# Attention values as a stationary block of high and low parts, in a two-layer kernel on one core

## The chip, the cores and the metric

One core of one Trainium2 chip runs the kernel. The metric is device time in microseconds (us) from one launch; lower is better. The times of before are the median of three runs.

## The reference

One block of a mixer, a gated feed-forward network and a per-layer embedding gate runs over 256 positions of width 2048 in fp32, then one layer of sliding-window attention with sinks. Only the attention layer's mixer is touched here:

```python
# D_MODEL 2048, 32 heads of 64, 4 key/value heads (8 query heads each), blocks of 128 positions
q, k, v, gate = split(h @ w_in, [2048, 2304, 2560])
q, k = rms_norm(q, q_gain), rms_norm(k, k_gain)       # per head of 64
s = einsum('bqhgd,bkhd->bhgqk', qj, kb) * scale + bias  # query block j, keys of blocks j-1 and j
s = where(valid, s, -inf)
m = maximum(max(s), sink)
p = exp(s - m)
p = p / (sum(p) + exp(sink - m))
o = einsum('bhgqk,bkhd->bqhgd', p, vb)
return (o * silu(gate)) @ w_out
```

So each query block weighs one or two blocks of 128 values, each head's row is divided by its denominator, and the result is multiplied by the silu of a gate and projected.

## The kernel before

Each engine has its own instruction stream, run strictly in order; semaphores tie them together.

**Large products.** All weights come in chunks of 256 rows by 512 columns (512 KB) through a ring of 8 buffers `w_raw`. To keep fp32 precision with faster products, each operand x is split into a high part (`w_hi`, rounded to the type F32R by ScalarE, L473) and a low part (`w_lo`, x minus high, by VectorE, L771). TensorE then issues three products 128x512 per piece: high times low, high times high, low times high (`chunk`, L1239 on; 12 products per chunk: 2 blocks of positions, 2 row blocks, 3 products). Split buffers are a ring of four (SPL), so ScalarE's split of chunk s waits until TensorE has used chunk s-4. Eight chunks are a *unit*, 512 output columns; it accumulates in two banks `acc`.

**The attention layer** has 9 units (SWA_UNIT + v, v = 0 to 8: keys and values, four of queries, four of gates), followed by 4 units of the output projection (SO_UNIT). The attention of a *group* g (8 query heads that share one key/value head) is spread by hand over units v = g+3 and g+4: in each engine's loop over v and chunk c, conditions such as `if c == 3 and 3 <= v <= 6` place a step behind the split or the product of chunk c. A group has three *rounds* r: round 0 is query block 0 with 8 heads and one key block; rounds 1 and 2 are query block 1, four heads each, two key blocks. For each round:
- `score` (TensorE, L1480) writes scores into the banks `sp`; `softmax_max` (VectorE, L1126 to L1134) scales them, adds the bias, takes the maximum; `exp` (ScalarE, L695, L697) follows, with the sums.
- `turn` (TensorE, L1279): eight 128x128 transposes of the probabilities into two halves of `tp`; ScalarE's `copy` (L518) takes them to `tile[7]`.
- `weigh` (TensorE, L1499): per head and key block one plain fp32 product, 128x128 probabilities stationary, 128x64 values moving, into one half of `tp`, with positions on partitions.
- `weighted` (VectorE, L1141 to L1148): denominator, reciprocal, and the multiply of that half by it into `wide`.

When the gate's unit is done, ScalarE takes it with Silu (L480), `gated` (L1156) multiplies it in, TensorE turns the result (`to_features`, L1269), and `high` (L488) and `low` (L779) split it into `yh` and `yl` for the output projection. The queries of each group are turned the same way and copied by ScalarE.

**The two halves of tp.** All transposes and weighed outputs pass through two banks, `tp[0]` and `tp[1]`, in the order of the list HALVES. Half h may be written once half h-2 has been taken (`free(h)`, `before(h)`), told by counters `tp_left["a"]` (ScalarE) and `tp_left["d"]` (VectorE); a letter in HALVES says who takes it ("x": ScalarE reads high, VectorE then takes low). In one unit the order is: turn(g,0) 2 halves, weigh(g,0) 1, turn(g,1) 2, queries of g+1 2, weigh(g,1) 1, turn(g,2) 2, weigh(g,2) 1.

**Order on TensorE in unit v = g+3**, behind chunk c: c=0 score(g,1); c=1 weigh(g-1,2); c=2 turn(g,0), score(g,2); c=3 weigh(g,0); c=4 turn(g,1); c=5 queries of g+1; c=6 score(g+1,0), weigh(g,1); c=7 turn(g,2).

**On ScalarE**, behind split c: c=0 query copy; c=2 copy of turn(g-1,2), exp(g,0); c=3 take of the last unit; c=4 exp(g,1); c=5 copy of turn(g,0); c=6 exp(g,2); c=7 copy of turn(g,1).

**On VectorE**, behind split c: c=1 weighted(g-1,1), softmax_max(g,0); c=3 softmax_max(g,1), weighted(g-1,2); c=5 softmax_max(g,2); c=6 weighted(g,0); c=7 the queries' mean squares.

Of the kernel before, what the change touches and what calls it, by code (L numbers as in the profile page):

```python
# [20 lines left out]
F32 = mybir.dt.float32  # L21
# [5 lines left out]
P = 128  # L27
# [57 lines left out]
for _g in range(5):  # L85
    if _g == 0:
        H_Q[0] = len(HALVES)
        HALVES += "aa"
        continue
    q = _g - 1  # L90
    H_PT[q, 0] = len(HALVES); HALVES += "aa"
    H_PV[q, 0] = len(HALVES); HALVES += "d"
    H_PT[q, 1] = len(HALVES); HALVES += "aa"
    if _g < 4:
        H_Q[_g] = len(HALVES); HALVES += "aa"
    else:
        H_OG[0] = len(HALVES); HALVES += "xx"
    H_PV[q, 1] = len(HALVES); HALVES += "d"
    H_PT[q, 2] = len(HALVES); HALVES += "aa"
    H_PV[q, 2] = len(HALVES); HALVES += "d"  # L100
for _g in range(1, 4):
    H_OG[_g] = len(HALVES); HALVES += "xx"
# [47 lines left out]
def build(nc, x, p, norm_mix_g, w_in, sgu_ln_g, sgu_ln_b, sgu_w, sgu_b, sc_conv_w, cf_conv_w,  # L150
# [11 lines left out]
    with ExitStack() as ctx:  # L162
# [100 lines left out]
        og_ready = sem("og_ready")  # L263
        last_bank = sem("last_bank")
# [202 lines left out]
        def _(act):  # L467
# [230 lines left out]

            for v in range(9):
                for c in range(8):  # L700
# [16 lines left out]
                    if (v, c) == (1, 3):  # L717
                        act.wait_ge(prod, 2)
                        take(SWA_UNIT, tok(0), ACT.Copy, rr)
                    if (v, c) == (2, 6):  # L720
# [3 lines left out]
                    if c == 0 and v >= 7:  # L724
                        high(H_OG[v - 7], yh[:, 4 * (v - 7):4 * (v - 7) + 4])

                    if c == 2 and 4 <= v <= 7:
                        copy(H_PT[v - 4, 2], tile[7])
# [4 lines left out]
                    if c == 3 and v >= 6:  # L733
                        if v > 6:
                            act.wait_ge(og_ready, v - 6)
                        take(SWA_UNIT + v - 1, tok(1), ACT.Silu, rr)
                    if c == 4 and 3 <= v <= 6:
                        exp(v - 3, 1)
                    if c == 5 and 3 <= v <= 6:
                        copy(H_PT[v - 3, 0], tile[7])  # L740
                    if c == 6 and 3 <= v <= 6:
                        exp(v - 3, 2)
                    if c == 7 and 3 <= v <= 6:
                        copy(H_PT[v - 3, 1], tile[7])

            for j in range(NG):
                for c in range(8):
                    split(START[SO_UNIT + j] + c)
                    if (j, c) == (0, 0):
                        high(H_OG[2], yh[:, 8:12])  # L750
                    if (j, c) == (0, 3):
                        act.wait_ge(og_ready, 3)
                        take(SO_UNIT - 1, tok(1), ACT.Silu, rr)
                    if (j, c) == (0, 5):
                        high(H_OG[3], yh[:, 12:16])
# [3 lines left out]
        def _(dve):  # L759
# [375 lines left out]

            def weighted(g, r):

                n = 3 * g + r
                t, h0, nh, nk = ROUNDS[r]
                dve.wait_ge(expd, n + 1)  # L1140
                step(dve.tensor_tensor(rden[:, n, 0:nh], ssum[:, n, 0:nh], ssink[:, n, 0:nh], ALU.add))  # L1141
                step(dve.reciprocal(rden[:, n, 0:nh], rden[:, n, 0:nh]))
                h = H_PV[g, r]
                wait_half(dve, h)
                dst = wide[:, t, CW * g + HD * h0:CW * g + HD * (h0 + nh)].rearrange("p (h n) -> p h n", n=HD)
                src = tp[h % 2][:, 0:HD * nh].rearrange("p (h n) -> p h n", n=HD)
                by = rden[:, n, 0:nh].unsqueeze(2).to_broadcast([P, nh, HD])
                dve.tensor_tensor(dst, src, by, ALU.mult).then_inc(tp_left["d"], 1)  # L1148

            def gated(g):  # L1150

                wait_left(dve, SWA_UNIT + 5 + g)
                cols = wide[:, :, CW * g:CW * (g + 1)]
                if g == 3:
                    wait_half_left(dve, H_PV[3, 2])
                dve.tensor_tensor(cols, cols, tok(1), ALU.mult).then_inc(og_ready, 1)  # L1156

            for v in range(9):
                for c in range(8):
# [22 lines left out]
                    if (v, c) == (2, 0):  # L1182

                        wait_left(dve, SWA_UNIT)
                        kv = tok(0)[:, :, 0:256]
# [14 lines left out]
                    if c == 0 and v >= 7:  # L1200
                        q = slice(4 * (v - 7), 4 * (v - 7) + 4)
                        low(H_OG[v - 7], yl[:, q], yh[:, q])
# [12 lines left out]
                    if c == 5 and 3 <= v <= 6:  # L1215
                        softmax_max(v - 3, 2)
                    if c == 6 and 3 <= v <= 6:
                        weighted(v - 3, 0)

            for j in range(NG):  # L1220
                for c in range(8):
                    split(START[SO_UNIT + j] + c)
                    if (j, c) == (0, 0):
                        low(H_OG[2], yl[:, 8:12], yh[:, 8:12])
                    if (j, c) == (0, 3):
                        gated(3)
                    if (j, c) == (0, 5):
                        low(H_OG[3], yl[:, 12:16], yh[:, 12:16])
# [9 lines left out]
        def _(pe):  # L1238
# [252 lines left out]
            def weigh(g, r):  # L1491

                t, h0, nh, nk = ROUNDS[r]
                wait_half_left(pe, H_PT[g, r] + 1)
                h = H_PV[g, r]
                free(h)
# [4 lines left out]
                last.then_inc(tp_ready, 1)  # L1501

            for v in range(9):
                for c in range(8):
# [26 lines left out]
                    if c == 5 and v >= 6:  # L1531
                        pe.wait_ge(og_ready, v - 5)
# [51 lines left out]
```

## Time and profile before

| | us |
|---|---|
| median of 3 runs | 1452.02 (1451.65 to 1453.01) |
| the profiled execution's own time | 1451.7 |
| its span, first to last instruction | 1449.7 |
| PE busy | 1443.1 |
| VectorE (DVE) busy | 961.3 |
| ScalarE (ACT) busy | 697.3 |

The profile is of one execution. PE is TensorE's products, PEld its weight loads, DVE VectorE, ACT ScalarE, POOL GpSimd; L12 is line 12 of the kernel. Busy does not mean at full rate: the records of pipelined products overlap, so a stretch is read by the distance of starts. The chain of waits gives a product's own share of time, from its start to the next start. The trace of HBM and DMA shows 188 GB/s over the span.

### The profile page before, as it was taken

The numbers are of one execution on the slowest core, as the hardware profiler recorded it, in microseconds if no ns is written. First come the engines' busy times: TensorE is split into PE (matmuls) and PEld (weight loads), VectorE is DVE, ScalarE is ACT, GpSimd is POOL, SyncE is SP. The second block draws the span as 40 slices with busy tenths as digits, with TensorE's granted clock in tenths as the row PEclk, the third lists the DMA queues.
The fourth block names the chain that finished last, engine by engine and source line by source line (L and its number), as shares of the span: only waits on it lengthen the run. The fifth ranks groups of instructions, "written<-read, shape, count | busy, mean of one in ns | idle before, by whom it ended". The sixth has DMA issues, their size and how long they took to land.

```text
span 1449.7 us, 18187 instructions
## 1 busy us (share of the span) xinstructions
PE 1443.1 (100%) x6679; PEld 1196.2 (83%) x6679; DVE 961.3 (66%) x1318; ACT 697.3 (48%) x926; POOL 51.4 (4%) x52
## 2 busy tenths in 40 slices
PE   9999999999999999999999999999999999999999
PEld 7888888888888888888888888888888888888887
DVE  5599977956666554566754546769798567665553
ACT  7444564454444433444444344445555566564432
POOL 2000010000000000000000000000000212200000
PEclk9999999999999999999999999999999999999999
DMA  9765556666665566666655666655565755545562
GB/s 334 221 189 175 182 178 217 190 195 186 198 197 194 189 191 195 195 190 192 195 188 190 193 197 190 194 185 179 196 202 176 235 152 171 154 125 164 173 206 89
DMA packets 141494, 274.03 MB, mean 189 GB/s; under 512 B 8593, under 2 KB 10893, under 8 KB 141304
## 3 DMA queue, kind: packets, MB, share of 16 engines
q1 hardware_dynamic: 139608, 266.49, 59.2%
q0 software_dynamic: 1792, 6.71, 1.5%
q8 instruction: 39, 0.64, 0.2%
q14 instruction: 23, 0.19, 0.0%
q10 hardware_dynamic: 32, 0.01, 0.0%
HBM read 271.02 MB, written 2.15 MB: 188 GB/s over the span
## 4 chain that ended last, share of the span: by engine, by line
PE 97%; DVE 1%; ACT 1%; issue 0%; POOL 0%; POOLq 0%; ACTq 0%
PE acc L1249 31%; PE acc L1251 30%; PE acc L1250 30%; PE tp L1499 1%; PE tp L1269 1%; PE acc L1311 1%; PE sp L1480 1%; PE tp L1279 1%; DVE w_lo L771 1%; DVE tile L1126 0%; ACT tile L695 0%; ACT w_hi L473 0%; DVE smx L1130 0%; PE acc L1286 0%; PE tp L1301 0%
## 5 line engine op out<-in xcount | busy, mean ns | idle before, releaser
L771 DVE TENSOR_TENSOR w_lo<-w_raw,w_hi 128x1024 fp32r<-128x1024 f32 x500 | 610.8, 1224 | 419.9 <-ACT w_hi L473 417.3
L473 ACT ACTIVATE w_hi<-w_raw 128x1024 fp32r<-128x1024 f32 x500 | 528.5, 1060 | 609.5 <-PE acc L1251 608.2
L1249 PE MATMUL acc<-w_lo,yh 128*128 128x512 f32 x1184 | 461.6, 390 | 0.0
L1251 PE MATMUL acc<-w_hi,yl 128*128 128x512 f32 x1184 | 460.7, 389 | 0.0
L1250 PE MATMUL acc<-w_hi,yh 128*128 128x512 f32 x1184 | 460.6, 389 | 0.0
L1249 PE MATMUL acc<-w_lo,hh 128*128 128x512 f32 x784 | 309.7, 395 | 0.0
L1251 PE MATMUL acc<-w_hi,hl 128*128 128x512 f32 x784 | 305.7, 390 | 0.0
L1250 PE MATMUL acc<-w_hi,hh 128*128 128x512 f32 x784 | 305.1, 389 | 0.0
L1249 PEld LDWEIGHTS acc<-w_lo,yh 128*128 128x128 f32 x1184 | 222.3, 188 | 46.3 <-issue 0.6
L1251 PEld LDWEIGHTS acc<-w_hi,yl 128*128 128x128 f32 x1184 | 222.3, 188 | 46.3
L1250 PEld LDWEIGHTS acc<-w_hi,yh 128*128 128x128 f32 x1184 | 222.3, 188 | 46.1
L1249 PEld LDWEIGHTS acc<-w_lo,hh 128*128 128x128 f32 x784 | 147.2, 188 | 32.0 <-issue 2.3
L1251 PEld LDWEIGHTS acc<-w_hi,hl 128*128 128x128 f32 x784 | 147.2, 188 | 31.4
L1250 PEld LDWEIGHTS acc<-w_hi,hh 128*128 128x128 f32 x784 | 147.4, 188 | 29.2
L795 DVE STREAM_TRANSPOSE tile<-resid 32x256 f32<-32x256 f32 x144 | 62.7, 436 | 2.3
L795 DVE STREAM_TRANSPOSE tile<-tile 32x256 f32<-32x256 f32 x128 | 55.8, 436 | 2.1
L849 DVE SCALAR_TENSOR_TENSOR tile<-tile,cw 128x255 f32<-128x255 f32 (+29 forms) x120 | 48.1, 461 | 0.0
L431 POOL TENSOR_SCALAR eps_ms<-ms 128x2 f32<-128x2 f32 (+2 forms) x9 | 8.4, 935 | 960.1 <-DVE ms L833 917.9
L695 ACT ACTIVATE tile<-tile,negm 128x128 f32<-128x128 f32 (+1 forms) x64 | 28.3, 444 | 20.8 <-DVE ssink L1134 20.8
L518 ACT ACTIVATE tile<-tp 128x512 f32<-128x512 f32 x32 | 17.2, 589 | 30.2 <-PE tp L1279 21.9
L480 ACT ACTIVATE tile<-acc,rs 128x512 f32<-128x512 f32 x42 | 26.3, 676 | 0.0
L827 DVE TENSOR_TENSOR resid<-acc,resid 128x512 f32<-128x512 f32 x38 | 24.3, 682 | 0.3 <-PE acc L1251 0.3
(150 smaller groups left out, 559.1 us busy)
## 6 DMA issues: line engine op xcount, KB each, us to landing
w_raw<-in_w_gate SPq DMA_DIRECT2D x88, 512.0 KB, 3.7
w_raw<-in_w_up SPq DMA_DIRECT2D x88, 512.0 KB, 3.8
w_raw<-in_w_down SPq DMA_DIRECT2D x88, 512.0 KB, 4.1
w_raw<-in_swa_w_in SPq DMA_DIRECT2D x72, 512.0 KB, 3.8
w_raw<-in_w_in SPq DMA_DIRECT2D x64, 512.0 KB, 4.3
w_raw<-in_w_out SPq DMA_DIRECT2D x32, 512.0 KB, 4.2
w_raw<-in_w_ple_gate SPq DMA_DIRECT2D x32, 512.0 KB, 3.7
w_raw<-in_swa_w_out SPq DMA_DIRECT2D x32, 512.0 KB, 4.0
```

The lines of the kernel that those rows point to most:

```text
L473: act.activation(w_hi[:, s % SPL], w_raw[:, s % RAW], ACT.Copy).then_inc(hi_ready, 1)
L480: last = act.activation(dst[:, t], acc[u % 2][t][:], func, scale=s_)
L518: act.activation(dst[:, 512 * i:512 * (i + 1)], tp[(h + i) % 2][:], ACT.Copy, scale=scale).then_inc(tp_left["a"], 1)
L695: act.activation(sv[:, i], sv[:, i], ACT.Exp, bias=negm[:, n, i:i + 1], accum_out=ssum[:, n, i:i + 1])
L771: dve.tensor_tensor(w_lo[:, s % SPL], w_raw[:, s % RAW], w_hi[:, s % SPL].bitcast(F32), ALU.subtract).then_inc(lo_ready, 1)
L795: last = dve.transpose(into, block)
L827: last = dve.tensor_tensor(cols, acc[u % 2][t][:], cols, ALU.add)
L849: dve.scalar_tensor_tensor(dst, src, w_, dst, ALU.mult, ALU.add).then_inc(conv, 1)
L1249: pe.matmul(dst, xh[:, f, tk], w_lo[:, s % SPL, k], start=(f == 0), stop=False)
L1250: pe.matmul(dst, xh[:, f, tk], w_hi[:, s % SPL, k], start=False, stop=False)
L1251: last = pe.matmul(dst, xl[:, f, tk], w_hi[:, s % SPL, k], start=False, stop=(f == CK * n - 1))
L1269: last = pe.transpose(half_tile(h + i)[:, k, P * t:P * (t + 1)], src[:, t, P * f:P * (f + 1)], ident[:])
```

## The change

The values are split once into a block per key block and value head: 64 columns of high parts and 64 of low parts side by side (`v_parts`, in part of `yh` that is free then), by ScalarE behind split (1, 5) and VectorE behind (2, 0). The turned probabilities are split too: `high` by ScalarE into `pt_hi` and `low` by VectorE into `pt_lo` replace ScalarE's copy. `weigh` now holds the value block stationary and moves 512 columns of probabilities (four heads by 128 positions), high then low part; the output comes with features on partitions: 0 to 63 from the values' high parts, 64 to 127 from the low parts. ScalarE copies the lower rows out (`keep_low_rows`), VectorE adds both (`weighted`) into `out_t`, already turned. Round 0 fills two halves of `tp` instead of one. The reciprocals of the denominators are no longer multiplied into the output but into the gate (`gated`), before the gate is turned; the turned gate is multiplied into the output (`og`), and ScalarE and VectorE split that (`og_high`, `og_low`).

```diff
+        pt_hi, pt_lo = yh[:, 12:16], yl[:, 12:16]
+        v_parts = yh[:, 8:12].rearrange("p (t a) (b n) -> p t (a b) n", t=T, n=P)
+        out_t = wide[:].rearrange("p t n -> p (t n)").rearrange("p (k n) -> p k n", k=KT)
# the list of halves: who takes them
-    H_PT[q, 0] = len(HALVES); HALVES += "aa"
-    H_PV[q, 0] = len(HALVES); HALVES += "d"
-    H_PT[q, 1] = len(HALVES); HALVES += "aa"
+    H_PT[q, 0] = len(HALVES); HALVES += "xx"
+    H_PV[q, 0] = len(HALVES); HALVES += "dd"
+    H_PT[q, 1] = len(HALVES); HALVES += "xx"
...
# ScalarE
+            def keep_low_rows(g, r):
+                for i in range(2 if r == 0 else 1):
+                    wait_half(act, H_PV[g, r] + i)
+                    act.activation(tile[7][0:HD, 512 * i:512 * (i + 1)], tp[(H_PV[g, r] + i) % 2][HD:P], ACT.Copy).then_inc(
+                        pv_low, 1)
+            def og_high(g):
+                act.wait_ge(og_ready, g + 1)
+                act.activation(yh[:, 4 * g:4 * g + 4], out_t[:, 4 * g:4 * g + 4], ACT.Copy).then_inc(og_hi, 1)
...
+                    if c == 1 and 4 <= v <= 7:
+                        keep_low_rows(v - 4, 1)
                     if c == 2 and 4 <= v <= 7:
-                        copy(H_PT[v - 4, 2], tile[7])
+                        high(H_PT[v - 4, 2], pt_hi)
...
                     if c == 4 and 3 <= v <= 6:
                         exp(v - 3, 1)
+                    if c == 4 and 4 <= v <= 7:
+                        keep_low_rows(v - 4, 2)
                     if c == 5 and 3 <= v <= 6:
-                        copy(H_PT[v - 3, 0], tile[7])
+                        high(H_PT[v - 3, 0], pt_hi)
                     if c == 6 and 3 <= v <= 6:
+                        keep_low_rows(v - 3, 0)
                         exp(v - 3, 2)
                     if c == 7 and 3 <= v <= 6:
-                        copy(H_PT[v - 3, 1], tile[7])
+                        high(H_PT[v - 3, 1], pt_hi)
# VectorE (denominators(g, r): the sum and reciprocal that weighted had)
             def weighted(g, r):
-                dve.tensor_tensor(dst, src, by, ALU.mult).then_inc(tp_left["d"], 1)
+                t, h0, _, _ = ROUNDS[r]
+                for i in range(2 if r == 0 else 1):
+                    dve.wait_ge(pv_low, 4 * g + (0, 2, 3)[r] + i + 1)
+                    bank_ = tp[(H_PV[g, r] + i) % 2][0:HD].rearrange("p (i e n) -> p i e n", i=2, e=2)
+                    low_ = tile[7][0:HD, 512 * i:512 * (i + 1)].rearrange("p (i e n) -> p i e n", i=2, e=2)
+                    at = 4 * g + h0 // 2 + 2 * i
+                    for e in range(2):
+                        last = dve.tensor_tensor(out_t[HD * e:HD * (e + 1), at:at + 2, P * t:P * (t + 1)], bank_[:, :, e],
+                                                 low_[:, :, e], ALU.add)
+                    last.then_inc(tp_left["d"], 1)
             def gated(g):
-                dve.tensor_tensor(cols, cols, tok(1), ALU.mult).then_inc(og_ready, 1)
+                dve.tensor_tensor(gate_, gate_, by, ALU.mult).then_inc(gate_ready, 1)
...
+                    if c == 2 and 4 <= v <= 7:
+                        low(H_PT[v - 4, 2], pt_lo, pt_hi)
+                        denominators(v - 4, 2)
                     if c == 3 and 3 <= v <= 6:
                         softmax_max(v - 3, 1)
-                    if c == 3 and 4 <= v <= 7:
+                        denominators(v - 3, 0)
+                    if c == 4 and 4 <= v <= 7:
                         weighted(v - 4, 2)
+                    if c == 5 and 3 <= v <= 6:
+                        low(H_PT[v - 3, 0], pt_lo, pt_hi)
+                        softmax_max(v - 3, 2)
+                        denominators(v - 3, 1)
+                    if c == 6 and 3 <= v <= 6:
+                        weighted(v - 3, 0)
+                    if c == 7 and 3 <= v <= 6:
+                        low(H_PT[v - 3, 1], pt_lo, pt_hi)
# TensorE
             def weigh(g, r):
-                for i in range(nh):
+                for i in range(2 if r == 0 else 1):
+                    h = H_PV[g, r] + i
+                    free(h)
                     for k in range(nk):
-                        last = pe.matmul(tp[h % 2][:, HD * i:HD * (i + 1)], tile[7][:, P * (nk * i + k):P * (nk * i + k + 1)],
-                                         tok(0)[:, k, 256 + HD * g:256 + HD * (g + 1)], start=(k == 0), stop=(k == nk - 1))
+                        for part in (hi_, lo_):
+                            ...
+                            last = pe.matmul(tp[h % 2][:], v_parts[:, k, g], probs, start=(k == 0 and part is hi_),
+                                             stop=(k == nk - 1 and part is lo_))
...
                     if c == 5 and v >= 6:
-                        pe.wait_ge(og_ready, v - 5)
-                        to_features(H_OG[g], wide[:, :, CW * g:CW * (g + 1)])
+                        pe.wait_ge(gate_ready, v - 5)
+                        to_features(H_OG[v - 6], tok(1))
```

Behind the gates' turns, `og` and `og_low` stand on VectorE at c=0 and c=1 of the following unit and `og_high` on ScalarE at c=1; the last gate is turned behind chunk 2 of the projection instead of chunk 3.

## Rows read from the trace of the kernel before

**Rows 1.** The page's busy times, share of the span, instructions.
```profile
PE 1443.1 (100%) x6679; PEld 1196.2 (83%) x6679; DVE 961.3 (66%) x1318; ACT 697.3 (48%) x926; POOL 51.4 (4%) x52
```

**Rows 2.** The waits of PE, whole span: total us, times, longest.
```profile
PE acc L1286 <- POOL ident L414: 1.6, 1, 1.6
PE acc L1311 <- ACT w_hi L473: 1.0, 1, 1.0
PE tp L1279 <- DVE wide L1148: 0.4, 1, 0.4
```

**Rows 3.** Stretches: length, busy PE, PEld, DVE, ACT, POOL, clock, DMA share, GB/s.
```profile
1239.28:1274.04 34.76, 34.76 (x210) 28.92 (x209) 23.05 (x46) 20.86 (x53) 5.97 (x4) 1.00 0.50 153
...
1318.42:1374.00 55.58, 55.58 (x258) 46.23 (x258) 31.77 (x30) 25.20 (x29) 0.00 (x0) 1.00 0.52 171
```

**Rows 4.** Chain that ended last, 1236 to 1275: start, time to the next piece.
```profile
1239.28 0.28 PE acc L1249
...
1242.11 0.87 PE tp L1279 x8
...
1245.75 1.06 PE sp L1480 x8
1246.81 0.43 PE acc L1249
...
1249.76 1.73 PE tp L1499 x16
...
1254.31 0.87 PE tp L1279 x8
...
1272.11 1.93 PE tp L1499 x16
```

**Rows 5.** Groups by line and shape, PE, whole span: busy, mean ns.
```profile
L1499 PE MATMUL tp<-tile 128*128 128x64 f32 x192 | 23.0, 273 | 0.0
```

**Rows 6.** Instructions in order of time, ACT: start, us; two stretches.
```profile
1243.65 0.41 ACT L695 ACTIVATE tile<-tile,negm 128x128 f32<-128x128 f32 x1
...
1252.47 0.51 ACT L695 ACTIVATE tile<-tile,negm 128x256 f32<-128x256 f32 x1 [2.49 <-DVE ssink L1134]
...
1254.55 1.04 ACT L473 ACTIVATE w_hi<-w_raw 128x1024 fp32r<-128x1024 f32 x1
1255.50 1.05 ACT L518 ACTIVATE tile<-tp 128x512 f32<-128x512 f32 x2
...
1286.19 1.28 ACT L695 ACT_TABLE_LOAD   x1
```

**Rows 7.** The same for DVE, three stretches with neighbours of one kind.
```profile
1077.22 1.80 DVE L795 STREAM_TRANSPOSE tile<-resid 32x256 f32<-32x256 f32 x4
...
1148.41 1.43 DVE L1198 TENSOR_TENSOR tile<-tile,rs 128x256 f32<-128x256 f32 x4 [1.56 <-POOL rs L433]
...
1303.26 1.29 DVE L779 TENSOR_TENSOR yl<-tp,yh 128x512 fp32r<-128x512 f32 x2 [0.98 <-ACT yh L488]
```

**Rows 8.** The same for DVE, 1239 to 1253.
```profile
1239.39 0.42 DVE L1148 TENSOR_TENSOR wide<-tp,rden 128x256 f32<-128x256 f32 x1 [2.51 <-PE tp L1499]
1239.73 2.15 DVE L1126 SCALAR_TENSOR_TENSOR tile<-sp,rs,big 128x128 f32<-128x128 f32 x8
...
1247.92 1.23 DVE L771 TENSOR_TENSOR w_lo<-w_raw,w_hi 128x1024 fp32r<-128x1024 f32 x1 [3.17 <-ACT w_hi L473]
1249.06 1.65 DVE L1126 SCALAR_TENSOR_TENSOR tile<-sp,rs,big 128x256 f32<-128x256 f32 x4
...
1252.35 0.15 DVE L1141 TENSOR_TENSOR rden<-ssum,ssink 128x4 f32<-128x4 f32 x1
...
1252.75 0.42 DVE L1148 TENSOR_TENSOR wide<-tp,rden 128x256 f32<-128x256 f32 x1
```

**Rows 9.** Unit 3: DVE in order of time, and PE's chain.
```profile
1192.18 1.22 DVE L771 TENSOR_TENSOR w_lo<-w_raw,w_hi 128x1024 fp32r<-128x1024 f32 x1
...
1194.49 0.66 PE tp L1279 x4
```

More of the change, by code:

```diff
@@ L263, in build @@
         og_ready = sem("og_ready")
+        v_hi = sem("v_hi")
+        v_lo = sem("v_lo")
+        pv_low = sem("pv_low")
+        gate_ready = sem("gate_ready")
+        og_hi = sem("og_hi")
+        og_lo = sem("og_lo")
         last_bank = sem("last_bank")
@@ L719, in _ @@
                         take(SWA_UNIT, tok(0), ACT.Copy, rr)
+                    if (v, c) == (1, 5):
+                        wait_left(act, SWA_UNIT)
+                        act.activation(v_parts[:, :, :, 0:HD], tok(0)[:, :, 256:512].rearrange("p t (g n) -> p t g n", n=HD),
+                                       ACT.Copy).then_inc(v_hi, 1)
                     if (v, c) == (2, 6):
@@ L1134, in softmax_max, with denominators @@
                 dve.tensor_tensor(ssink[:, n, 0:nh], snk, smx[:, n, 0:nh], ALU.subtract).then_inc(smax, 1)
-            def weighted(g, r):
[L1138 to L1147, printed above, removed]
-                dve.tensor_tensor(dst, src, by, ALU.mult).then_inc(tp_left["d"], 1)
+            def denominators(g, r):
+                n = 3 * g + r
+                _, h0, nh, _ = ROUNDS[r]
+                den = rden[:, 3 * g + (r > 0), h0:h0 + nh]
+                dve.wait_ge(expd, n + 1)
+                step(dve.tensor_tensor(den, ssum[:, n, 0:nh], ssink[:, n, 0:nh], ALU.add))
+                step(dve.reciprocal(den, den))
@@ L1150, in gated @@
             def gated(g):
                 wait_left(dve, SWA_UNIT + 5 + g)
[L1153 to L1156 removed]
+                by = rden[:, 3 * g:3 * g + 2].unsqueeze(3).to_broadcast([P, T, HG, HD])
+                gate_ = tile[1][:].rearrange("p (t h n) -> p t h n", t=T, h=HG)
+                dve.tensor_tensor(gate_, gate_, by, ALU.mult).then_inc(gate_ready, 1)
@@ new lines, in og, with og_low @@
+            def og(g):
+                for i in range(2):
+                    wait_half(dve, H_OG[g] + i)
+                    dst = out_t[:, 4 * g + 2 * i:4 * g + 2 * i + 2]
+                    last = dve.tensor_tensor(dst, dst, half_tile(H_OG[g] + i), ALU.mult)
+                    last.then_inc(tp_left["d"], 1)
+                dve.wait_ge(tp_left["d"], sum(1 for i in range(H_OG[g] + 2) if taker(i) == "d"))
+                dve.engine_nop().then_inc(og_ready, 1)
+            def og_low(g):
+                dve.wait_ge(og_hi, g + 1)
+                q = slice(4 * g, 4 * g + 4)
+                dve.tensor_tensor(yl[:, q], out_t[:, q], yh[:, q].bitcast(F32), ALU.subtract).then_inc(og_lo, 1)
@@ L1200, in _ @@
                     if c == 0 and v >= 7:
-                        q = slice(4 * (v - 7), 4 * (v - 7) + 4)
-                        low(H_OG[v - 7], yl[:, q], yh[:, q])
+                        og(v - 7)
+                    if c == 1 and v >= 7:
+                        og_low(v - 7)
                     if c == 1 and 4 <= v <= 7:
@@ L1214, in _ @@
                         gated(v - 6)
[L1215 to L1218, printed above, removed]
             for j in range(NG):
@@ L1223, in _ @@
                     if (j, c) == (0, 0):
-                        low(H_OG[2], yl[:, 8:12], yh[:, 8:12])
+                        og(2)
+                    if (j, c) == (0, 1):
+                        og_low(2)
                     if (j, c) == (0, 3):
                         gated(3)
+                    if (j, c) == (0, 4):
+                        og(3)
                     if (j, c) == (0, 5):
-                        low(H_OG[3], yl[:, 12:16], yh[:, 12:16])
+                        og_low(3)
                     if j and c == 3:
```

50 lines of the change are left out of this document (25 added, 25 removed).

## The prediction

> **What bounds the kernel now.** I read the page's busy times first: PE is busy for the whole span [rows 1], so only what shortens PE's stream, or makes PE wait, can move the time. Then PE's waits: three of them matter and together they are 3.0 us, the longest 1.6 us and two at the start; in the attention stage PE waits once, 0.4 us, for the scaled output of group 0 [rows 2]. Then the stage by stretches: between two groups PE is busy for all 34.76 us at full clock, DVE for 23 and ACT for 21 [rows 3]. So PE alone is the limit there, but DVE and ACT run in order and hand work to each other, and the change lengthens their hand-overs. Its worth must come from a walk along the three queues.
>
> I call T the end of the PE pass weigh(g-1, 1) and the start of chunk 7, 1239.28 in [rows 4]. From T to the next T PE issues 8 chunks (2.77 us each; 2.95 behind a score, 2.83 behind a weigh), 3 turns and one turn of the queries (0.87 each), 3 scores (1.06, 1.06, 1.09) and 3 weighs (1.73, 1.73, 1.93) [rows 4]. The sum is 34.76 us, the stretch of [rows 3].
>
> **What PE gains.** A weigh of before has 8 fp32 products 64 wide, each two records (192 records in 12 weighs) [rows 5], and takes 1.73 us, or 1.93 behind a score. A new one has 4 products of 512 columns of the split type, in every round: round 0 has two banks, one key block, two parts; rounds 1 and 2 one bank, two key blocks, two parts. A chunk has 12 such products in 2.77 us, so 4 take 0.92. The first product behind the fp32 ones takes 0.28 instead of 0.23 [rows 4], 0.05 more is gained. So each weigh gains 0.81 + 0.05 = 0.86 to 0.87 us, and 12 of them 10.4 us. Bounds for one product: 0.23 (the chunk's) and 0.39 (the whole length of a chunk's record if nothing overlapped, which the spacing of the chunks speaks against); I take 0.23. Turns and scores stay as they are; the output turns only change their source.
>
> **What is added on ACT and DVE.** ACT's copy of a turned bank becomes high(), same size, same 0.59 and 0.50 apart [rows 6]. New on ACT is keep_low_rows, 64x512 from the bank, four per group: bounds 0.41 (an exp of 128 columns [rows 6]) and 0.67 (DVE's length for 512 columns from a bank, below); I take the 0.59 of the plain 512-column copy, since it reads as many columns. New on DVE: low() of both banks of each turn, two in 1.29 us, so 0.67 each with their overlap, and the next instruction can start 1.22 after their start [rows 7]; three pairs are 3.7 us per group. weighted() was one multiply (0.42; in round 0 twice the columns, some 0.67); it is now two adds of 64x256 per bank, 8 per group. An add of 256 columns is 0.42 long. Spacing: four 256-wide products into the same partitions stand in 1.43 us, one every 0.34, so each starts before its predecessor is done; four transposes that each write another quarter of the partitions stand in 1.80 us, one every 0.45 with 0.44 of length, no overlap [rows 7]. The new adds write partitions 0-63 and 64-127 in turn, so I take 0.445 each, and keep 0.34 and 0.49 as ends (the latter 0.41 a piece of the four bias products' 1.65 [rows 8], plus the same 0.08 of lost overlap). The Trainium skill, VectorE: DVE Perf Modes, section "Two Vector instructions with no wait between them", says in general that an instruction whose output starts in another quadrant than the last is held until all earlier ones are finished; the trace agrees with it in these two rows. Were the adds to overlap in spite of it, the forecast would be 2.5 us lower.
>
> DVE gets 3.7 + 8 x 0.445 - 1.5 = 5.8 us more per group, 29 of some 35: not full. ACT gets 4 x 0.5 = 2. Where it counts is who waits in which order.
>
> **The wait that the change makes.** A half of tp can be written once the half two places before it is left. The second half of turn(g, 0) stands two places behind H_PV[g-1, 2], so PE waits there for weighted(g-1, 2). Before, DVE did it straight behind softmax_max(g, 1): 1252.75 plus 0.42, and PE came to that turn at 1254.31 [rows 4, 8]; 1.6 us to spare. Now ACT must first copy the lower rows, and keep_low_rows(g-1, 2) stands on ACT behind exp(g, 1), which itself waits for softmax_max(g, 1). DVE's weighted has moved behind split 4 and waits for the copy.
>
> The chain from T, step by step [rows 6, 8]:
> - T to ACT's copy 0.11 (DVE's start at 1239.39), copy 0.59, hand-over 0.05, two adds 0.89: softmax_max(g, 0) starts at T+1.64. Before, it was T+0.45: the copy of round 1 is in the chain too.
> - start of softmax_max(g, 0) to that of exp(g, 0): 1239.73 to 1243.65, 3.92. Thence to DVE's split 3, which waits for ACT's split 3 behind all of exp: 1247.92, 4.27. To softmax_max(g, 1): 1249.06, 1.14. To exp(g, 1): 1252.47, 3.41. Exp itself: 1254.55, 2.08. Sum 14.82, so ACT's copy starts at T+16.46.
> - copy 0.59, hand-over 0.05, two adds 0.445 + 0.42: PE is released at T+18.0 (0.04 to PE).
>
> Denominators(g, 0), split 2, the low() of round 2 and split 4 lie in DVE's waits for ACT inside this chain (3.17 before split 3 [rows 8]) or in exp(g, 1)'s 2.08, so they cost nothing; they would if they were over some 1.5 us longer.
> PE, without waiting, comes there at T + 2.77 + 0.87 + 2.77 + 1.06 + 2.95 + 0.92 + 2.77 + 0.44 = T+14.55. It waits 3.5 us. Behind a wait the four transposes take 0.66 and not 0.44 [rows 9], 0.22 more.
>
> Then DVE is late for turn(g, 1), whose second half wants weighted(g, 0). From softmax_max(g, 0)'s start: ACT's split 5 behind the copy ends at 16.4, DVE's split 5 takes to 17.55, low() to 18.8, softmax_max(g, 2) to 22.05, the denominators 0.40 (1252.35 to 1252.75), split 6 to 23.6, four adds end at 25.4. PE comes to this half at 25.2 (16.4 + 0.66 + 1.06 + 2.95 + 0.92 + 2.77 + 0.44). Wait 0.2, restart 0.22.
> Period: 34.76 - 2.61 + 3.5 + 0.22 + 0.2 + 0.22 = 36.3 us against 34.76: **+1.5** in units 4 and 5. Unit 6 has two table loads; the second ends at 1287.47 [rows 6], where exp would have begun at 1252.47 + 34.75 = 1287.22: 0.25 more, +1.8.
>
> Unit 3 has no earlier group, but low(H_PT[0, 0]) (1.22) and the denominators of round 1 (0.40) come in front of split 6, which began at 1192.18; four adds behind it end at 1192.18 + 1.62 + 1.14 + 1.76 = 1196.70, PE goes on at 1196.74 instead of 1194.49 [rows 9], +2.25, and gains 0.87 in weigh(0, 1): **+1.4** at the first T (weigh(0, 0)'s gain is lost in this wait).
> Behind the last T only weigh(3, 2) is left, -0.87: turn(4, 0) doesn't exist. In units 7 and 8 and in the output projection DVE is busy 32 of 56 us [rows 3]; og, og_low and the gate's multiply (1.2 us each) lie in its idle time, two to three chunks ahead of who wants them. If this cover were gone each would cost its 1.2. The split of the values (0.6 on ACT, 0.7 on DVE) comes a unit before its first use.
>
> Sum: 1.4 + 2 x 1.5 + 1.8 - 0.9 = +5.3 us on the profiled execution's 1451.7 (span 1449.7 and 2.0 around it), 1457.0. The median of the runs is 0.3 above that execution: **1457.3 us**. The same as books: PE gains 10.4, loses some 15.7 in waits.
>
> **Its range.** Low ends of all unknown costs (copy 0.41, adds every 0.34) take 0.4 + 0.55 from a group, 1454 in all; high ends (copy 0.67, adds 0.49, 0.25 for a product) add 0.15 + 0.25 + 0.2, 1459.5. The likeliest case has 1454.5 to 1460.
>
> **Rivals.**
> - The gain arrives, the waits don't: PE's stream shrinks by 10.4 us, and ACT gets to the lower rows in time. For it: PE is the only full engine, DVE and ACT have 5 us free per group. Against: exp(g, 1) stands in front of the copy on ACT, and it can't start before softmax_max is done. It would need the chain to be 3.5 us shorter; the change is a gain as soon as both waits of a group together are under 2.6 us. Time 1452.0 - 10.4 = 1441.6.
> - The chain holds, but the adds and copies are cheap (64 partitions being cheaper than 128, or overlap), or restarts cost nothing: +0.5 per group and less. 1452 to 1454.5.
> - DVE becomes the bound: low() takes over the turn's bank and strided adds from a bank take 0.67 each (the length for 512 columns). Then weighted(g, 0) ends 1.0 later and both others 0.5, 2 us more per group, about half of it in unit 3: about 1463. Against it: 256-wide rows with a bank as input are 0.42.
> - The clock. Granted clock is 1.00 in the stretches of [rows 3], and PE has never waited over 1.6 us [rows 2]; three waits of 3.5 us are new. If after each one chunk ran at 1.2 instead of 2.4 GHz, 2.77 us more each, the time would be 1465 to 1466. The Trainium skill, TensorE: Matmul & The Clock Gate, section "HAM oscillation", names idle gaps between bursts of matmuls as what brings the clock down; no row here shows a gap as long as those that I forecast.
> - The change doesn't do what it says: the block with high and low parts as stationary is loaded at each product and is not hidden. A load is 0.19 and a chunk's product takes 0.23 with one behind it, so this has little for it; 0.19 x 4 in the two weighs of the chain would be +1.5 per group, 1463.
>
> **Chances.** Forecast 0.60, gain arrives 0.12, cheap chain 0.12, DVE the bound 0.09, clock 0.04, load not hidden 0.03. What a measurement can tell from no change is about 0.2%, 2.9 us, so "slower" begins at 1454.9. Slower: 0.56 of the forecast's 0.60, and the last three, 0.16: 0.72. Within: 0.04 + 0.11 = 0.15. Faster: 0.13. The range leaves out the first rival and the far end of the last ones: 1452.5 to 1462.
>
> **What would show it.** In the changed trace: three waits of PE at turn(g, 0) of about 3.5 us, put down to weighted's add; four small ones at turn(g, 1), the first of 2 to 3 us; weighs of 0.92; stretches between two T of 36.3 us; PE's busy time about 10 us lower. The keep_low_rows of round 2 directly behind exp(g, 1)'s last piece. I am wrong if the stretch is under 34.7, if the copy runs before exp, or if the wait is put down to another half of tp.

## The result and the profile after

The kernel after takes 1461.75 us (1460.73 to 1464.14, 6 runs) against 1452.02 (1451.65 to 1453.01, 6 runs): 1.0068 times as long, 95% interval 1.0058 to 1.0078. The change costs 9.7 us where +5.3 was forecast. The profiled execution took 1461.6 us, its span is 1459.6, 9.9 more than before's. 1461.75 lies inside the range that was given, 1452.5 to 1462, at its very end.

The page of after, busy times as in [rows 1]:

```profile
PE 1439.7 (99%) x6535; PEld 1187.7 (81%) x6535; DVE 989.5 (68%) x1367; ACT 707.5 (48%) x939; POOL 53.6 (4%) x52
```

There are 144 records of PE fewer, as counted (192 of the small products give way to 48), but its busy time fell by 3.4 us only, not by some 10. So the records that are left must have become longer. The waits of PE over the whole span of after, the view of [rows 2] (total us, times, longest):

```profile
PE tp L1345 <- DVE wide L1181: 13.3, 5, 3.9
...
PE tp L1573 <- DVE yl L806: 1.2, 1, 1.2
```

The first line is new in size: PE waits five times before half of a turn (L1345 is L1279 of before) for `weighted`'s add (L1181), 13.3 us in all. Three of these waits, 3.66, 3.64 and 3.86 us, stand before the second half of turn(g, 0) in groups 1 to 3; the other two, 1.96 and 0.16, before the halves of turn(0, 1) in unit 3. The chain of waits through the first of them (start, time to the next piece); T is 1206.36 here:

```profile
1205.22 1.14 PE tp L1573 x4
...
1206.38 0.60 ACT tile L713
...
1207.44 0.42 DVE wide L1181
...
1207.89 2.17 DVE tile L1153 x8
...
1213.66 1.34 ACT tile L705 x7
...
1215.10 0.96 ACT w_hi L483
...
1217.38 1.58 DVE tile L1153 x4
...
1221.12 1.66 ACT tile L705 x7
...
1222.90 0.60 ACT tile L713
...
1223.52 0.42 DVE wide L1181
...
1223.95 0.43 DVE wide L1181
...
1224.42 1.11 PE tp L1345 x4
1225.54 2.01 PE sp L1546 x8
1227.55 0.72 PE acc L1315
1228.27 0.43 PE acc L1316
...
```

This is the forecast's chain link by link (some links are left out above): ACT's copy of the lower rows, the adds, softmax_max(g, 0), exp, split 3, softmax_max(g, 1), exp(g, 1), and only then the copy that `weighted` wants. PE is released at T+18.06; the forecast said T+18.0. But read the last four rows. The four transposes take 1.11 us, not the 0.66 that followed the wait in [rows 9]; a score takes 2.01, not 1.06; and the chunk's products stand up to 0.43 apart, not 0.23. Stretches of after (length, busy PE, PEld, DVE, ACT, POOL, clock, DMA share, GB/s): three from T to T, as in [rows 3], then the time from each release to the next weigh, then 2 us inside the first of these and 2 us at its end, past the start of the weigh:

```profile
1206.36:1244.66 38.30, 34.64 (x173) 27.36 (x173) 28.71 (x57) 23.16 (x57) 6.88 (x4) 0.91 0.43 136
1244.66:1282.12 37.46, 33.82 (x173) 26.75 (x173) 28.62 (x57) 23.16 (x57) 6.87 (x4) 0.95 0.46 141
1282.12:1318.47 36.35, 32.49 (x157) 25.86 (x157) 30.98 (x60) 25.75 (x58) 0.00 (x0) 0.95 0.38 114
1224.42:1231.54 7.12, 7.12 (x25) 5.20 (x26) 6.20 (x14) 2.16 (x4) 0.96 (x1) 0.63 0.37 118
1262.73:1269.00 6.27, 6.27 (x25) 4.61 (x26) 6.05 (x14) 2.15 (x4) 0.95 (x1) 0.73 0.39 130
1300.39:1306.66 6.27, 6.27 (x25) 4.60 (x26) 6.05 (x14) 2.15 (x4) 0.00 (x0) 0.73 0.52 161
1226.00:1228.00 2.00, 2.00 (x9) 1.18 (x6) 1.30 (x4) 1.12 (x2) 0.00 (x0) 0.50 0.59 145
1230.00:1232.00 2.00, 2.00 (x10) 1.65 (x9) 1.86 (x7) 0.00 (x0) 0.51 (x1) 1.00 0.22 76
```

The granted clock at each long wait goes to 0.50, that is 1.2 GHz, and then back to 1.00, 2.4 GHz. In the first case it fell before the wait's end, at about 1222.9, and stayed at 0.50 until about 1229.7; in the other two it fell 1.0 to 1.1 us after PE had gone on and stayed low for 3.4 us. At full clock the same work (transposes 0.66, score 1.06, chunk 2.95) takes 4.67 us. It took 7.12, 6.27 and 6.27: 2.45 + 1.6 + 1.6 = 5.65 us lost.

The first and third of the same three stretches in before, around the one of [rows 3]:

```profile
1204.53:1239.28 34.75, 34.75 (x209) 28.91 (x209) 23.05 (x46) 20.86 (x53) 5.97 (x4) 1.00 0.52 153
...
1274.04:1307.50 33.46, 33.46 (x193) 28.01 (x193) 24.34 (x48) 23.36 (x55) 0.00 (x0) 1.00 0.41 116
```

Where the span's 9.9 us are: the first T comes 1.83 later (1206.36 against 1204.53); the three stretches from T to T, the *periods*, last 38.30, 37.46 and 36.35 against 34.75, 34.76 and 33.46, so +3.55, +2.70 and +2.89; from the last T to the end it is 141.1 against 142.2, -1.1.

### The profile page after: what moved, and what is told of

The parts are those of the page before. It is cut to its first block, busy times and chain, and to the rows that moved or that the text cites. A ratio compares the mean times of both kernels' runs of the same rounds, so it can differ in the third digit from the quotient of the medians.

```text
span 1459.6 us, 17963 instructions
## 1 busy us (share of the span) xinstructions
PE 1439.7 (99%) x6535; PEld 1187.7 (81%) x6535; DVE 989.5 (68%) x1367; ACT 707.5 (48%) x939; POOL 53.6 (4%) x52
## 4 chain that ended last, share of the span: by engine, by line
PE 94%; DVE 3%; ACT 2%; issue 1%; POOL 0%; POOLq 0%; DVEq 0%; ACTq 0%
PE acc L1315 30%; PE acc L1316 29%; PE acc L1317 29%; PE tp L1335 1%; PE acc L1377 1%; ACT tile L705 1%; DVE tile L1153 1%; DVE w_lo L798 1%; DVE smx L1157 1%; PE sp L1546 1%; PE tp L1573 1%; ACT w_hi L483 1%; PE tp L1345 1%; DVE wide L1181 0%; ACT tile L713 0%
## 5 line engine op out<-in xcount | busy, mean ns | idle before, releaser
L1345 PE MATMUL tp<-ident,tile 128*128 128x128 f32 x108 | 15.4, 280 | 13.3 <-DVE wide L1181 13.3
L1345 PEld LDWEIGHTS tp<-ident,tile 128*128 128x128 f32 x108 | 12.7, 143 | 16.2 <-DVE wide L1181 12.3
```

The lines of the kernel that those rows point to most:

```text
L1345: last = pe.transpose(tp[(h + i) % 2][:, P * (b % 4):P * (b % 4 + 1)], src(b), ident[:])
```

## The experiments

The theory after the result (A): the wait at turn(g, 0) costs as forecast, and the fall of the clock behind it makes the rest. A rival (B): what is slow behind the wait has another cause, or the period's surplus is DVE's or ACT's amount of work and stays when the order is changed. Each kernel below was timed in four to eleven runs, beside runs of before on the same chip; its ratio is to those. The figures behind a time are the lowest and highest run, those in brackets the 95% interval of the ratio. Beside each run's time the mean granted clock of its whole span is on record; it is 0.995 or 0.996 in all six runs of after, and 1.000 in every run of before beside the kernels below.

**Fill the wait.** In turn(g, 0) of groups 1 to 3, 20 small products of the identity with itself, into a score bank that is free then, stand on PE between the two halves. They add work that the result doesn't need.

```diff
+ pe.wait_ge(scored, n + 2)
+ for _ in range(20):
+     pe.matmul(sp[0][:, 0:P], ident[:], ident[:], start=True, stop=True)
  free(h + 1)    # then the transposes of the second half
```

> PE's wait at the second half of turn(g, 0) stays where it is, but 20 small products (128 columns, some 0.15 us each, into a score bank that is free by then) fill it, so PE is busy nearly all the time. Theory (the trace's 4.3 us beyond my sum are the clock: granted 0.50 for some 5 us behind each of three waits of 3.7 to 3.9 us): products behind the wait are 0.23 apart again, the stretches between two T fall from 38.3, 37.5 and 36.4 to about 36.3, 36.3 and 35.2, the time to about 1457.4, some 4 us under the changed kernel. Rival (the slower products come from something else at that place, such as the restart of the queue or VectorE's and ScalarE's traffic there): they stay 0.43 apart and the time stays within 1 us of 1461.7, or grows.

Measured 1458.9 us (1457.7 to 1459.3), ratio 1.0047 [1.003, 1.0063]. Stretches of it, first 2 us in unit 3 (group 0, whose turn the edit leaves as it is), then the three periods:

```profile
1198.00:1200.00 2.00, 2.00 (x7) 1.52 (x6) 2.00 (x4) 1.33 (x2) 0.00 (x0) 0.50 0.70 220
1207.92:1244.36 36.44, 36.44 (x214) 30.24 (x213) 28.62 (x57) 23.17 (x57) 6.87 (x4) 1.00 0.46 143
...
1244.36:1280.86 36.50, 36.50 (x214) 30.27 (x213) 28.63 (x57) 23.17 (x57) 6.87 (x4) 1.00 0.46 145
1280.86:1316.08 35.22, 35.22 (x197) 29.37 (x197) 30.88 (x60) 25.76 (x58) 0.00 (x0) 1.00 0.37 117
```

PE has more to do and the periods are shorter: 36.44, 36.50 and 35.22, together 3.95 us less than after's, all at full clock. So A holds: the falls come with PE's idleness, and filling it keeps the clock up. The products filled 4.47 us, so that the second half of the turn began at T+18.90, 0.84 later than in after, and took 0.44 instead of the 0.66 behind a wait; 5.65 - 3 x (0.84 - 0.22) = 3.8 us should be won, and 3.95 were. (That the periods come near those of the prediction, 36.3, 36.3 and 35.2, is in part chance: the filling is 0.84 longer than the wait, and PE has no waits at turn(g, 1), which the prediction had put at 0.42 a group.) The first row is a miss of both theories: in unit 3, which the edit doesn't touch, the clock fell this time behind two waits of 1.2 and 2.0 us, and T came at 1207.92 instead of 1206.36. In after's profile it did not fall there. That cost 1.6 of the 3.95, and the span is 2.4 shorter. The median missed the expected 1457.4 by 1.5, for which such a fall is the likely but not the shown cause: the runs took 1459.3, 1459.1, 1458.7 and 1457.7 at a mean clock of 0.999, 0.999, 0.998 and 1.000.

**ScalarE's copy ahead of exp.**

```diff
  # ScalarE, behind split 4
+ if 4 <= v <= 7: keep_low_rows(v - 4, 2)
  if 3 <= v <= 6: exp(v - 3, 1)
- if 4 <= v <= 7: keep_low_rows(v - 4, 2)
```

> One swap on ScalarE: keep_low_rows(g-1, 2) goes in front of exp(g, 1). Theory (two chains: the wait at turn(g, 0) is ScalarE's order, but the period is set by VectorE's queue up to weighted(g, 0)): VectorE's weighted(g-1, 2) now starts behind split 4, at T+15.8, PE is released at T+16.7 after a wait of about 2.2 us; that is too short for the clock to fall, as 1.96 us was in unit 3; then turn(g, 1) waits about 1 us for weighted(g, 0), so the period is 35.8, not shorter. Time about 1455.7. Rival (the one wait was all): period 34.3 and less, time 1451 to 1452. Rival (clock falls all the same): over 1459.

Measured 1457.45 (1456.28 to 1461.6), 1.0048 [1.0032, 1.0065]. This is 1.8 over the 1455.7 expected. The copy no longer waits behind exp(g, 1), but `weighted` stands on DVE behind softmax_max(g, 1) and split 4, and PE still waits 2.3 us at turn(g, 0). PE in order of time, the second halves of two turns, one group apart (start, us, [idle before <- releaser]):

```profile
1223.06 0.66 PE L1345 MATMUL tp<-ident,tile 128*128 128x128 f32 x4 [2.29 <-DVE wide L1181]
...
1258.76 0.65 PE L1345 MATMUL tp<-ident,tile 128*128 128x128 f32 x4 [2.27 <-DVE wide L1181]
```

and the two periods around them:

```profile
1206.36:1242.06 35.70, 32.59 (x173) 25.71 (x173) 28.43 (x57) 23.27 (x57) 6.88 (x4) 1.00 0.46 148
1242.06:1278.10 36.04, 33.77 (x173) 26.79 (x173) 28.45 (x57) 23.05 (x57) 6.87 (x4) 0.95 0.47 145
```

Two waits that are alike to 0.02 us, in one execution: behind the first the clock stayed at 1.00, behind the second it fell. The third wait at this place, in unit 6, is the longest of the three, and behind it the clock stayed at 1.00 too:

```profile
1295.93 0.66 PE L1345 MATMUL tp<-ident,tile 128*128 128x128 f32 x4 [3.43 <-DVE wide L1181]
```

So the length of one wait doesn't decide it alone. Over the attention stages of all the traces here, the clock fell at or behind 5 of the 7 waits of 3.3 to 3.9 us (3 of 3 in after, none of 1 here, 2 of 3 in the kernel with the adds in the same rows, below) and 7 of the 14 of 1.67 to 2.3 us. That goes with the spread of this kernel's runs over 5 us: 1456.3, 1456.6, 1458.3 and 1461.6 us at a mean clock of 0.999, 0.998, 0.996 and 0.995.

**The same, and DVE's weighted directly behind softmax_max(g, 1)**, ahead of denominators(g, 0) and split 4.

> The swap on ScalarE, and weighted(g-1, 2) on VectorE directly behind softmax_max(g, 1), where the kernel before had it. Theory (VectorE's queue is the bound): PE's wait at turn(g, 0) falls to 0.6 us, the one at turn(g, 1) grows to about 2.5, the period stays 35.8 and the time that of the swap alone, 1455.7, within 1 us. Rival (each wait counts by itself): another 1.5 us less per group, 1451 to 1452.

Measured 1459.27 (1455.87 to 1460.73), 1.0047 [1.003, 1.0063], no better, and 3.6 over the expected 1455.7. PE waits 0.71 at turn(g, 0), as hoped, but then 0.18 at the weigh and 1.74 at turn(g, 1), which wants weighted(g, 0), and there the clock falls, in two of the three groups:

```profile
1233.82:1236.40 2.58, 2.58 (x7) 1.99 (x7) 2.58 (x5) 1.54 (x2) 0.00 (x0) 0.50 0.82 275
```

The wait was moved, not taken away: the next link in order was late by what PE had gained. What is missing to the expectation is the clock: the one run of this kernel at a mean clock of 1.000 took 1455.87, the three at 0.998, 0.998 and 0.996 took 1459.1, 1459.4 and 1460.7.

**All steps in the order of need.** Beside the above, weighted(g, 0) stands ahead of softmax_max(g, 2), the low() of round 1 ahead of split 6 and denominators(g, 1) behind it; ScalarE's high() of round 1 ahead of exp(g, 2).

```diff
  # VectorE, behind split 5
  low(H_PT[v - 3, 0], pt_lo, pt_hi)
+ weighted(v - 3, 0)
  softmax_max(v - 3, 2)
- denominators(v - 3, 1)
+ low(H_PT[v - 3, 1], pt_lo, pt_hi)
  # behind split 6: denominators(v - 3, 1) instead of weighted(v - 3, 0)
```

> Besides both moves of before: weighted(g, 0) stands in front of softmax_max(g, 2), low() of turn(g, 1) behind it and in front of split 6, denominators(g, 1) behind split 6; on ScalarE the high() of turn(g, 1) stands in front of exp(g, 2). Theory (the waits are the order of the queues, not the amount of work on VectorE): no wait at turn(g, 1), some 0.5 us at the turn of the queries, period about 33.5, unit 3 better by 2 us; time 1446 to 1449, faster than before. Rival (VectorE has too much work): a new wait of 2 us or more appears at splits 6 or 7 or at the turn of the queries, time 1452 or more.

Measured 1457.71 (1456.64 to 1458.43), 1.004 [1.0026, 1.0054]: 8.7 us over the upper end of the expected 1446 to 1449. The first period is 35.74 and the wait at turn(g, 0) 2.3 again. The chain of waits says why; it no longer runs through the copies:

```profile
1201.44 1.14 DVE ms L1135
...
1202.67 1.11 POOL eps_ms L441
...
1203.85 2.30 POOL rs L443
1206.15 1.56 issue
1207.71 2.17 DVE tile L1152 x8
```

softmax_max(g, 0) wants the scale of the queries, which DVE's mean squares (L1135, behind split 7) and GpSimd (5.1 us from the squares' end to the use) make. The 1.56 of "issue" is not DVE's: in the list of instructions GpSimd's second step, a power, lasts 3.77 us here, till 0.09 before DVE's start. In before, in after and in the next kernel it lasts 2.90 to 2.93; why it is longer here stays open. With softmax_max sooner in all other places, this ring was what came last.

**The same, with the queries' mean squares behind split 4** instead of split 7.

> The rebalanced order, with VectorE's query_stats behind split 4 instead of split 7. The rebalanced kernel's chain of waits ran from query_stats through GpSimd's reciprocal root (1.1 + 2.3 + 1.6 us) into the next softmax_max(g, 0), so its period of 35.7 us was a ring through VectorE, ScalarE and GpSimd, not PE's. Theory (each ring that is cut uncovers the next shorter one, all of them made of exp in front of a split on ScalarE): the ring through GpSimd is gone, the period is about 34.2, short waits of 0.2 to 0.6 us at turn(g, 0), weigh(g, 0), the turn of the queries and chunk 6; time 1448 to 1451. Rival (the period is VectorE's amount of work): it stays at 35 or over, 1455 and more.

Measured 1451.69 (1451.46 to 1453.27, 10 runs), 0.9998 [0.9988, 1.0008]: 6 us less for one moved call, and the slowdown is gone. (Expected were 1448 to 1451.) Part of the 6 us is the clock's: it fell behind two of the three waits of 2.25 us in the kernel before this one, and in this one every run has a mean clock of 1.000. Every wait of PE is now under 1.3 us but for the one at the start (PE's waits, as above):

```profile
PE tp L1572 <- DVE yl L805: 3.1, 4, 1.2
PE tp L1344 <- DVE wide L1180: 2.1, 3, 0.7
PE acc L1314 <- DVE w_lo L797: 1.9, 4, 0.5
PE acc L1351 <- POOL ident L424: 1.6, 1, 1.6
```

**Each exp behind the next split.** On ScalarE exp(g, 0) moves behind split 3, exp(g, 1) behind split 5 and exp(g, 2) behind split 7, so that DVE gets its splits and isn't made to wait behind an exp.

```diff
- if c == 2 and 3 <= v <= 6: exp(v - 3, 0)
+ if c == 3 and 3 <= v <= 6: exp(v - 3, 0)
- if c == 4 and 3 <= v <= 6: exp(v - 3, 1)
+ if c == 5 and 3 <= v <= 6: exp(v - 3, 1)    # then high() of round 0
- if c == 6 and 3 <= v <= 6: exp(v - 3, 2)    # behind the two that stand there
+ if c == 7 and 3 <= v <= 6: exp(v - 3, 2)
```

> As the one with early query_stats, and on ScalarE each exp stands behind the following split: split 3, exp(g, 0); split 5, exp(g, 1); split 7, exp(g, 2). VectorE's split 3 no longer waits for all of exp(g, 0), which takes 2.7 us out of the chain from T to softmax_max(g, 1); PE should find everything ready: period 32.2, no wait in units 4 to 6, no fall of the clock, time 1441 to 1443. Rival (VectorE at 29 of 32 us can't keep in step): waits of 1 us and more at turn(g, 1) or at a split, 1446 and more.

Measured 1444.57 (1444.4 to 1445.42), 0.9949 [0.9932, 0.9965], 1.6 over the upper end of what was expected. The same kernel once more, beside other runs of before:

> The version with splits in front of exps once more, next to the two others on one chip, for a narrower interval: 1444.5, 7 us under before; every theory so far expects the same.

Measured 1444.65 (1444.43 to 1446.41), 0.995 [0.9936, 0.9964]. This version beats both kernels, by 7 us and by 17. The page, the largest of PE's waits and one period of it:

```profile
PE 1434.1 (99%) x6535; PEld 1183.9 (82%) x6535; DVE 990.3 (69%) x1367; ACT 706.8 (49%) x939; POOL 50.9 (4%) x52
```

```profile
PE acc L1314 <- DVE w_lo L797: 1.9, 4, 0.5
```

```profile
1203.01:1235.83 32.82, 32.35 (x174) 25.81 (x173) 28.52 (x57) 22.93 (x57) 5.97 (x4) 1.00 0.49 162
```

DVE and ACT are as busy as in after (990.3 and 706.8 against 989.5 and 707.5) with 17 us less time. That refutes the second half of B: the surplus was the order of the steps, not their amount. The filled wait had refuted the first half. The period is 1.93 under before's 34.75, of 2.6 that the three weighs free.

**ScalarE's order alone** (after, with the copy behind split 4 and the exps behind splits 3, 5 and 7; DVE's order untouched).

> The changed kernel with ScalarE's order alone mended: keep_low_rows(g-1, 2) behind split 4, exp(g, 0), exp(g, 1), exp(g, 2) behind splits 3, 5, 7; VectorE and PE as changed. Theory (ScalarE's order is the cause; VectorE's new work and order are affordable): PE waits about 0.5 us at turn(g, 0) and 0.7 at the turn of the queries, period 33.3, clock as before, 1446 to 1449. Rival (VectorE's order, weighted behind split 4 and split 6, is as much to blame): the period stays over 34.8, 1452 or more.

Measured 1446.88 (1446.76 to 1447.72), 0.9964 [0.995, 0.9978], as expected. The first period is 33.15 (33.3 expected), at clock 1.00:

```profile
1204.62:1237.77 33.15, 32.42 (x173) 25.69 (x173) 28.43 (x57) 23.05 (x57) 6.88 (x4) 1.00 0.51 159
```

Most of the mend, 15 of 17 us, is thus on ScalarE, the falls of the clock that it avoids included: exp(g, 0) and exp(g, 1) no longer stand in front of splits 3 and 5, nor exp(g, 1) in front of the copy, so DVE gets its inputs sooner. How the gain divides among the four moved steps no run here shows, but for the copy alone, above.

**Control: before, with its exps behind splits 3, 5 and 7.** Is the gain of the mended kernels the change's, or had before room as well?

> Control: the kernel before with ScalarE's exps behind splits 3, 5 and 7, nothing of the change. Theory (the order is worth something only because the change uses up the slack; before, PE waits 0.4 us in the whole stage): 0.4 to 0.6 us less than before, 1451.2 to 1451.5, hardly to be told from it. Rival (the order is a gain of its own, and the gain of the mended kernels is not the change's): 1446 or less.

Measured 1451.06 (1450.83 to 1451.34, 11 runs), 0.9993 [0.9984, 1.0002]. The order is worth 0.7 us at most in before, within the noise. So some 6.4 us of the mended version's 7.1 are the change's own gain. DVE's new order was not tried in before, but PE waits there only once, 0.4 us, in the attention stage [rows 2], so it can't be worth much more.

**The low() of round 1 behind split 6** in the best version.

> The version with splits in front of exps, and low() of turn(g, 1) behind split 6 instead of in front of it. Its waits of 0.47 us (and 0.27 of restart) at chunk 6's split should go; instead the turn of the queries may wait up to 0.5 us for the second half of low(). Theory (two hand-overs of the same size, one replaces the other): 1444 to 1444.8. Rival: all of it goes, 1442.

Measured 1445.85 (1445.67 to 1447.2), 0.9955 [0.9941, 0.9968], 1.2 slower, where the same time or a little less was expected. The 0.5 us waits for split 6 go, and PE now waits four times at the turn of the queries (L1334) for low() of round 1 to free the half of `tp` that it wants, 0.9 each:

```profile
PE tp L1334 <- DVE yl L805: 3.6, 4, 0.9
```

**Adds into the same rows.** In groups 0 to 2 the second add of each pair writes partitions 0 to 63, into the place of the next group, instead of 64 to 127; a part of the output is then missing.

```diff
- out_t[HD * e:HD * (e + 1), at:at + 2, ...]
+ out_t[0:HD, at + 4 * e:at + 4 * e + 2, ...]    # g < 3
```

> The changed kernel, but in groups 0 to 2 the second add of each pair writes partitions 0 to 63 like the first, into the place of the next group (so half of the output of these groups is missing and overwritten). Theory (an instruction whose output starts in another part of the partitions than the last one is held until the engine is empty): the adds stand 0.34 us apart instead of 0.43, four in 1.45 us instead of 1.73; the chain is shorter by 0.3 us per group, the time by about 1 us, 1460 to 1461. Rival (the spacing is what 64-row operands with a bank cost): four stay at 1.73.

Measured 1459.74 (1458.81 to 1460.79), 1.0049 [1.0033, 1.0066]. The same two instants in DVE's order of time, of after and then of this kernel (each one its own profile):

```profile
1223.52 0.85 DVE L1181 TENSOR_TENSOR wide<-tp,tile 64x256 f32<-64x256 f32 x2 [1.28 <-ACT tile L713]
...
1232.67 1.73 DVE L1181 TENSOR_TENSOR wide<-tp,tile 64x256 f32<-64x256 f32 x4
```

```profile
1224.58 0.75 DVE L1182 TENSOR_TENSOR wide<-tp,tile 64x256 f32<-64x256 f32 x2 [1.28 <-ACT tile L713]
...
1233.82 1.41 DVE L1182 TENSOR_TENSOR wide<-tp,tile 64x256 f32<-64x256 f32 x4 [0.35 <-ACT tile L713]
```

With an add 0.42 long, two in 0.85 start 0.43 apart and two in 0.75 start 0.33 apart. Of these adds only the place that is written differs. The three waits at turn(g, 0) are 3.35, 3.31 and 3.53 us, 0.31 to 0.33 shorter than in after, as the 0.3 per group expected. The time shows less: its runs, 1458.8, 1458.9, 1460.6 and 1460.8 us, go with mean clocks of 0.996, 0.996, 0.995 and 0.995; in the profiled execution the clock fell in unit 3 and behind the first and third of these waits, not behind the second. The Trainium skill, VectorE: DVE Perf Modes, section "Two Vector instructions with no wait between them", says that an instruction whose output begins in another quadrant of partitions than the last one's is held till all earlier ones have ended; this pair of traces agrees, 0.10 us per add.

## Why the prediction was right and wrong

- *PE's gain*: right. Four split products take 0.92 in the weigh at 1231.54 and at 1269.00, and in the version without waits 1.93 of the 2.6 us per group arrive.
- *The chain to the second half of turn(g, 0)*: right, place, links and time (T+18.06 for T+18.0). The waits were 3.64 to 3.86 for 3.5, since PE came there at T+14.40 to T+14.43 for T+14.55; in unit 6 the release was 0.2 later, at T+18.27, as forecast for its table loads.
- *The adds 0.445 apart*: right (0.43), and for the reason given, as the kernel with the adds in the same rows showed.
- *The small waits at turn(g, 1)* (0.42 a group): not seen. In after PE comes there late by its slow stretch, so they don't arise, and no run of this order shows them at full clock. (In the version with ScalarE's copy first, 0.66 and 0.16 us stand there in a period at full clock.)
- *Unit 3*: +1.4 forecast, +1.83 measured. PE was released into the last half of turn(0, 1) at 1197.10 for 1196.74: split 6, which the walk had beginning 1.62 later than in before, began 2.00 later (1194.18), DVE standing idle for 0.27 of it behind the reciprocal. PE's wait of 1.19 at weigh(0, 0), for low() of round 0, cost nothing: the wait of 1.96 behind it took it up.
- *Behind the last T*: -1.1 for -0.9; the gate's steps were covered as said.
- *The clock*: here the prediction was wrong. The sum was made at full clock for what follows a wait of 3.5 us (4.67 us from the release to the weigh) and added only 0.22 for the restart. It took 6.27 to 7.12. So the failed step is the term for the granted clock behind the three long waits, which the forecast had at nothing. It was a rival with a chance of 0.04, priced at 2.77 for each wait. The price was too high: it measured 2.45, 1.6 and 1.6, together 5.65. Of that 3 x 0.42 came back, because the small waits at turn(g, 1) didn't arise. The three periods, 112.1, are 4.3 over the forecast's 107.8, and 5.65 - 1.26 = 4.4. The chance was far too low: the mean clock was below 1 in every run of after. The argument against it, that no row shows such a gap, was an argument for not knowing. The Trainium skill, TensorE: Matmul & The Clock Gate, section "HAM oscillation", which the prediction weighed, says that idle gaps between bursts of matmuls bring the clock down. The trace of after agrees in three cases of three, the filled wait from the other side; over all traces here two waits of 3.3 and 3.4 us went by without a fall.

The sum again: +1.8 before the first T, +1.5, +1.5 and +1.8 for the periods as forecast, 4.4 for the clock less the small waits, -1.1 behind the last T: +9.9, the span's difference. The chain of waits was right, and the omitted term is the clock's. That 1461.75 still fell within the range is luck: the range's upper part was there for other rivals, and the likeliest case had ended at 1460. The first rival, that the gain arrives if the waits don't (1441.6), names what the change is worth in another order: 1444.6 was reached.

What stays open: why the clock fell behind one wait of 2.3 us and not behind its like, nor behind one of 3.43, and what the last 3 us to 1441.6 want; 1.9 of them are the four waits for split 6, and moving these made others.

## What to carry to other kernels

When a forecast puts a new wait of several us into a stream of products that never paused, price the clock behind it: look for the slowest level that a row at that clock would give, and give it the better part of the chance, not a remainder. A change that takes work off the full engine and puts hand-overs onto the others must come with a new order of the steps there: walk each queue from the release that the full engine wants backwards, and put long steps that nobody waits for (here exp) behind short ones that somebody does (the splits). After each mend read the chain anew, since the next ring (here the queries' scale through GpSimd) may be just behind; the first three versions still had waits of 1.7 us and more and stood 2.5 to 4.3 us under after, the next two steps gave 6 and 7 more.

## What the runs showed of the hardware

- With waits of 3.66, 3.64 and 3.86 us PE's granted clock went to 0.50, for 3.4 us in two cases and 6.8 in one (from inside the wait on), with 512-column products 0.43 apart instead of 0.23; the losses were 2.45, 1.6 and 1.6 us. Behind waits of 3.31 and 3.43 us it stayed at 1.00, behind waits of 2.3 us it fell in one group and not in the next, and with 1.2 and 2.0 us in one profile and not in another. The shortest wait with a fall was 1.74 us. 20 small products in the gap kept it at 1.00 in three cases of three.
- A period got shorter when useless products were added to the engine that bounds it: 38.30 to 36.44 us.
- DVE's adds of 64x256 start 0.33 us apart into the same partitions and 0.43 into alternating ones.
- GpSimd's two steps for the queries' scale, a multiply-add and a power on 128x16, take 1.10 and 2.90 to 2.93 us in after; in the version with all steps in the order of need the power took 3.77.
